# Modulation partials summed over partitions with ones as weights, in four column groups of TensorE

## What is computed

```
# first block, layer l
ada = silu(c) @ w_ada[l] + b_ada[l]                 # (1, 6 * 1024)
sh1, sc1, g1, sh2, sc2, g2 = split(ada, 6)
h = x * (1 + sc1) + sh1
...
# second block, layer l: 9 * 1024 columns, for two vectors
mod_x = ada_params(c, w_ada[l], b_ada[l])           # for the tokens
mod_c = ada_params(c_ctx, w_ada[l], b_ada[l])       # for the context
```

## Time and profile before

| | us |
|---|---|
| median of 3 runs | 2823.49 |
| lowest and highest | 2822.88, 2828.95 |
| the profiled execution | 2827.61 |
| its span | 2825.8 |
| DVE busy in it | 1769.0 |
| ACT busy in it | 1086.2 |
| POOL busy in it | 226.9 |

### The profile page before, as it was taken

One profiled execution on the slowest core, in us unless ns is written; L12 is line 12 of the kernel. 1 busy time (PEld: TensorE's weight loads), 2 busy tenths in 40 slices (PEclk: granted clock), 3 DMA queues, 4 the chain that ended last, 5 costly groups with the idle time before them and its releaser, 6 DMA issues. The chain is left out here.

```text
span 2825.8 us, 40791 instructions
## 1 busy us (share of the span) xinstructions
PE 2630.3 (93%) x15939; PEld 2259.5 (80%) x15939; DVE 1769.0 (63%) x3184; ACT 1086.2 (38%) x2068; POOL 226.9 (8%) x170
## 2 busy tenths in 40 slices
PE   4768999999998999999999999999999999989999
PEld 4748998968998688887765778888788888777999
DVE  6567776657777656545759675554555533668754
ACT  2243544444443433323338233322333322446553
POOL 2000100001000211101000021110111100100110
PEclk8868999868999999999999999999999999999999
DMA  8924874914765244332620334433244433522653
GB/s 295 261 89 139 265 250 151 271 46 152 238 230 186 75 135 148 131 123 90 164 88 2 120 100 154 135 127 112 91 148 145 138 124 116 147 75 84 215 176 124
DMA packets 354873, 413.80 MB, mean 146 GB/s; under 512 B 24737, under 2 KB 291914, under 8 KB 354618
## 3 DMA queue, kind: packets, MB, share of 16 engines
q1 hardware_dynamic: 352496, 404.13, 44.8%
q0 software_dynamic: 832, 4.65, 0.5%
q10 hardware_dynamic: 1354, 2.43, 0.2%
HBM read 409.56 MB, written 5.27 MB: 147 GB/s over the span
## 5 line engine op out<-in xcount | busy, mean ns | idle before, releaser
L683 DVE TENSOR_TENSOR weight_lo<-raw_weights,weight_hi 128x512 fp32r<-128x512 f32 x1024 | 774.6, 763 | 886.0 <-ACT weight_hi L1242 873.9
L1242 ACT ACTIVATE weight_hi<-raw_weights 128x512 fp32r<-128x512 f32 x1024 | 635.6, 631 | 1326.7 <-PE bank L895 1203.9
L895 PE MATMUL bank<-H_hi,weight_hi 128*128 128x256 f32 (+1 forms) x2832 | 967.6, 342 | 71.3 <-POOL H_lo L853 46.3
L895 PE MATMUL bank<-H_lo,weight_hi 128*128 128x256 f32 (+1 forms) x2832 | 947.8, 335 | 0.0
L895 PE MATMUL bank<-H_hi,weight_lo 128*128 128x256 f32 (+1 forms) x2832 | 947.4, 335 | 0.0
L895 PEld LDWEIGHTS bank<-H_hi,weight_hi 128*128 128x128 f32 x2832 | 548.9, 194 | 156.9 <-issue 75.9
L895 PEld LDWEIGHTS bank<-H_hi,weight_lo 128*128 128x128 f32 x2832 | 549.5, 194 | 50.6
L895 PEld LDWEIGHTS bank<-H_lo,weight_hi 128*128 128x128 f32 x2832 | 550.2, 194 | 47.7 <-issue 1.0
L1545 DVE SCALAR_TENSOR_TENSOR ada_partial<-raw_weights,silu_c,ada_partial 128x512 f32<-128x512 f32 x616 | 441.1, 743 | 1.7 <-issue 0.4
L895 PE MATMUL bank<-hidden_hi,weight_hi 128*128 128x256 f32 (+1 forms) x1056 | 358.7, 340 | 3.2 <-DVE weight_lo L683 3.2
L895 PE MATMUL bank<-hidden_hi,weight_lo 128*128 128x256 f32 (+1 forms) x1056 | 354.9, 336 | 0.0
(11 more groups left out here) (172 smaller groups left out, 2169.4 us busy)
## 6 DMA issues: line engine op xcount, KB each, us to landing
raw_weights<-in_w_ada_dram SPq DMA_DIRECT2D x120, 1024.0 KB, 5.3
raw_weights<-in_w_ffn_up_dram SPq DMA_DIRECT2D x88, 1024.0 KB, 5.5
raw_weights<-in_w_ffn_in_dram SPq DMA_DIRECT2D x44, 1024.0 KB, 5.9
raw_weights<-in_w_ffn_down_dram SPq DMA_DIRECT2D x32, 1024.0 KB, 5.2
raw_weights<-in_w_in_dram SPq DMA_DIRECT2D x18, 1024.0 KB, 6.0
raw_weights<-in_w_ffn_out_dram SPq DMA_DIRECT2D x16, 1024.0 KB, 7.7
raw_weights<-in_w_in_ab_dram SPq DMA_DIRECT2D x12, 1024.0 KB, 10.0
raw_weights<-in_w_in_cd_dram SPq DMA_DIRECT2D x12, 1024.0 KB, 8.2
```

Of the source, the lines that this page charges most:

```text
L683: eng.tensor_tensor(WL[:, p.g % SPLIT, 0:p.kt * CW].rearrange("p (t n) -> p t n", n=CW), raw_ap(ch.n, ch.kt, CW)[:, p.k0:p.k0 + p.kt, :], ...
L895: return pe.matmul(o, w, x, start=start, stop=stop, skip_group_check=True)
L1242: act.activation(WH[:, p.g % SPLIT, 0:p.kt * CW].rearrange("p (t n) -> p t n", n=CW), raw_ap(ch.n, ch.kt, CW)[:, p.k0:p.k0 + p.kt, :], ACT ...
```

## The change

`sum_rows` swaps the operands and the layout. The stationary operand is now a block of ones, 32 columns wide, and the partials are moved, 128 of them per call. Each of the four calls of a vector writes into its own 32 partitions of the bank, 32q to 32q + 31: the columns 32q to 32q + 31 of each of the four blocks of 128. So every one of these 32 partitions holds the same sums, lying along the free axis. The number of calls stays at 4 or 8.

`columns` turns them upright. A tensor_reduce with a transpose inside blocks of 32 x 32 adds up the 32 equal rows and puts the 32 results on the partitions, into the first 4 or 8 columns of the group's own `ACC`, which is free by then. DVE waits for its end (`chain.link`), and then a scalar_tensor_tensor multiplies by 1/32 and adds the bias.

```diff
--- before.py
+++ after.py
@@ -917,10 +917,11 @@
             if g > 0:
 
                 pe.wait_ge(ada_out, g)
-            for j in range(AW // P):
-                for v in range(nv):
-                    ins = mm(B_ADA[:, j * nv + v:j * nv + v + 1],
-                             ACC[:, g % 2, v, j * P:(j + 1) * P], ones[:, 0:1], True, True)
+            for v in range(nv):
+                part = ACC[:, g % 2, v, :].rearrange("p (j q i) -> p j q i", q=4, i=32)
+                for q in range(4):
+                    o = B_ADA[32 * q:32 * q + 32, P * v:P * v + P].rearrange("p (j i) -> p j i", i=32)
+                    ins = mm(o, ones[:, 0:32], part[:, :, q, :], True, True)
             ins.then_inc(ada_sum, 1)
 
         def wait_bank(at, f):
@@ -1571,12 +1572,16 @@
             bias = (B1 if m < 2 else B2)[:, m % 2, :]
             dve.wait_ge(ada_sum, g + 1)
             b = bias[:, n * at:n * at + n]
+            col = ACC[:, g % 2, 0, 0:n * nv]
+            chain.link(dve.tensor_reduce(col, B_ADA[:, 0:P * nv].rearrange("p (c i) -> p c i", i=32), AX.X, ALU.add,
+                                         apply_transpose=True))
             if nv == 2:
                 b = b[:, :, None].broadcast_to([P, n, 2])
-                o, i = AD[m][:, n * at:n * at + n, :], B_ADA[:, 0:2 * n].rearrange("p (c v) -> p c v", v=2)
+                o, i = AD[m][:, n * at:n * at + n, :], col.rearrange("p (v c) -> p c v", v=2)
             else:
-                o, i = AD[m][:, n * at:n * at + n, 0], B_ADA[:, 0:n]
-            dve.tensor_tensor(o, i, b, ALU.add).then_inc(ada_out, 1)
+                o, i = AD[m][:, n * at:n * at + n, 0], col
+            dve.scalar_tensor_tensor(out=o, in0=i, scalar=1.0 / 32, in1=b, op0=ALU.mult, op1=ALU.add
+                                     ).then_inc(ada_out, 1)
 
         def setup():
             dve.memset(ZERO[:, :], 0.0)
```

## The result

The kernel with the change takes 2804.64 us (median of 5 runs, 2795.43 to 2807.25) where the kernel before took 2828.94 in the runs beside it (5 runs, 2822.88 to 2832.91): a ratio of 0.9911, with an interval of 0.9889 to 0.9934, or 19 to 31 us less. Two later repetitions gave 0.9889 and 0.9907. The forecast of 2796 is a ratio of 0.9903 to the 2823.49 it started from. The profiled execution has a span of 2802.8 us, 23.0 less than before.

The account below looks back on a forecast made before the run. PE was taken to bound the kernel; 30.5 us saved on its sums less 2.3 paid on DVE made 28.2 off the 2825.8 us span, 2797.6, hence a forecast median of 2796, range 2789 to 2811.

Parts of the forecast that it names:

- The sum on PE: In 20 one-vector and 23 two-vector modulation sums: 0.34 and 1.03 us saved each, 30.5 us together.
- the lower end of the range: 2789 us: a third of the layout cost absent in the 43 sums, 43 x 0.15 = 6.5 us.
- Rival 1: In the sums on PE: records no faster than 0.053 us each, saving 14.1 in all, 2809.4 us; chance 0.15.
- Rival 2: In every sum: four calls not run at once, 12.0 us lost on PE, 2.3 on DVE, 2837.8; chance 0.05.
- The reduce: On DVE in each group: a plain reduce's time, adding 0.45 or 0.32 us, 22.8 us of work in all.
- rival 3: In the DVE loop: a reduce takes 1.7 us rather than 0.42, costing 8.8, 2801.8 us; chance 0.10.
- Where DVE sets the time: From 738 to 862 us, DVE's loop pays the reduce in full: 5 x 0.45 = 2.3 us.
- The attention entries: Before attention stages: PE waits for the last column step, but the shorter sum's 0.34 or 1.03 covers 0.32 or 0.45.
- The DVE work outside the DVE-bound cycles: Mostly hidden in the counted stretches, behind PE's cover of three weight pieces: 4.3 us at 256 columns, 8.2 at 512.

Follow-up runs that it names:

- no_reduce: The kernel after without the transposing reduce and the factor 1/32, DVE adding the bias to the bank's first columns; 2794.20 us, ratio 0.9872.
- reduce_only: The kernel before with the transposing reduce and its wait added on DVE, PE's sum left as it was; 2834.21 us, ratio 1.0030.

## Why the prediction was right, and where it was off

**The sum on PE** (1.79 to 0.76, 0.88 to 0.54). Right: 0.78 and 0.55. Both parts of it were seen apart: passes of four records some 0.11 us apart, and 0.30 us per visit with narrow weights (0.26 to 0.30 by the cycles), where the prediction had 0.33. Measured from sum to sum the saving is 0.96, not 1.03, and 0.33, not 0.34: 23 x 0.07 + 20 x 0.01 = 1.8 us less than forecast. Two of the prediction's figures don't come out of its rows, without harm to the forecast: a record of the old sum costs 1.79 / 16 = 0.112 us and not 0.106, and the 0.15 us at the lower end of the range is nearly half of the layout cost and not a third.

**The rivals on PE.** Rival 1, records at 0.053 us each, is refuted: sixteen of them span 0.64 us. The Trainium skill gives a floor of about 25 ns from start to start (TensorE: Matmul & The Clock Gate, Wait — 56ns, not 53.3ns?). Between calls into different column groups the trace doesn't bear it out: two records run in the window 1043.08:1043.09 and four in 1043.10:1043.11, so four starts lie within 0.03 us. Only the mean over the passes, one record per 0.027 us, is near it. Rival 2 did not happen, but the run with one column group showed its price: 42.6 us from the kernel after, against 42.5 in the prediction (30.5 + 12.0).

**The reduce.** Forecast as a plain one, 419 and 285 ns; the groups of DVE after (busy us, mean ns, idle before):

```profile
L1576 DVE TRANSPOSE_TENSOR_REDUCE ada_partial<-bank 128x8 f32<-128x256 f32 x28 | 12.3, 439 | 0.0
...
L1576 DVE TRANSPOSE_TENSOR_REDUCE ada_partial<-bank 128x4 f32<-128x128 f32 x32 | 9.9, 309 | 2.5 <-PE bank L895 1.8 <-DVE X L1728 0.2
```

That is 20 and 24 ns over these (the plain reduce of 128 elements read SBUF, this one PSUM), and rival 3 falls. The Trainium skill's one element per cycle and lane for the transposing array (Vector Engine (DVE) Microarchitecture Reference, The reshape front-end and per-opcode configuration) fits the trace as far as it goes: 128 elements more take 130 ns more, about 1 ns each.

**Where DVE sets the time.** Right in place and mechanism, a little small in size: 0.57 us per cycle on average instead of 0.45. The timeline shows 0.49 of it, the reduce and the gap to the instruction that waits for its end; the other 0.08 isn't traced. The four cycles that repeat make 2.3 us. A fifth like them would make it 2.8 where the prediction had 2.3, but the stretch from sum 27 to 29 doesn't show it (132.40 to 133.59 us before, 132.14 to 134.36 after).

**The attention entries.** Wrong. The prediction let the shorter sum pay for the reduce there. PE's timeline after, at two of these places:

```profile
1460.48 1.99 PE L895 MATMUL bank<-k,q 64*128 64x512 f32 x8 [2.27 <-DVE ada L1583]
...
2504.18 3.65 PE L895 MATMUL bank<-k,q 64*128 64x512 f32 x8 [2.13 <-DVE ada L1583]
```

Before, PE waited 1.78 us at both for the values' copies on ACT; the second place then:

```profile
2526.10 1.99 PE L895 MATMUL bank<-k,q 64*128 64x512 f32 x8 [1.78 <-ACT v L1373]
```

The sum had long been done, so its length didn't count; DVE comes to the columns only behind its low part, and the step is now the last to arrive: 0.49 and 0.35 us more.

The two entries of the first block pay as well, though the profile names ACT's copy there. Before and after, DVE's column step and then PE:

```profile
576.56 0.15 DVE L1579 TENSOR_TENSOR ada<-bank,b_ada_cols 128x4 f32<-128x4 f32 x1
576.81 0.93 PE L895 MATMUL bank<-k,q 64*128 64x128 f32 x8 [1.63 <-ACT v L1373]
```

```profile
572.55 0.16 DVE L1583 SCALAR_TENSOR_TENSOR ada<-ada_partial,b_ada_cols 128x4 f32<-128x4 f32 x1
572.82 0.93 PE L895 MATMUL bank<-k,q 64*128 64x128 f32 x8 [1.98 <-ACT v L1374]
```

PE starts 0.10 and 0.11 us behind the end of the column step, and 0.4 to 0.8 behind the end of the copy: here the step was the last to arrive even before. The wait is longer by 0.35. At the other entry (sum 8) the sum does stand right ahead of it, as the prediction had it, and the wait went from 0.84 to 1.62 us: 0.42 for the shorter sum, which PE can't use, and 0.36 for the reduce. In no_reduce the four waits are 1.26, 1.62, 1.78 and 1.78 us. So the reduce costs about 1.5 us at the four entries, where the prediction had nothing. With four reduces the longest of these waits is 3.7 us, as the step's length on the path demands.

**Together.** 30.5 - 1.8 - 2.3 - 1.5 = 24.9 us by the measured terms (24.4 with a fifth DVE-bound cycle), and about 25 in the profiles without the stage whose clock varies; the prediction had 28.2. The three timed ratios make 25, 31 and 26 us of 2824. The close agreement of the sum is worth less than it looks: the three regular stretches hold 20 of the 23 two-vector and 8 of the 20 one-vector sums and show 21.9 us, and in the other stretches terms of a few tenths stand beside chance of several us.

The DVE work outside the DVE-bound cycles was called hidden, and one reduce is nearly so (no_reduce's median is 3.8 us lower, less than the two intervals can tell apart; 2.3 and 1.5 make 3.8). What the prediction didn't say is how thin the cover is at 256 columns; it took three pieces of weights as 4.3 us, and the fourfold reduce found 0.4 left behind the first.

**Left open.** Why reduce_only pays 8 us, 2 to 15 by its interval, where the traced terms add up to 4.6 to 6.5; whether taking the columns late is a gain of 2 us; and what decides how long PE stays at 1.2 GHz in the second layer's attention.

## What to carry to other kernels

An fp32 record cost PE 0.11 us, whether it loaded 128 columns and moved one, loaded 32 and moved 128, or loaded and moved 128; with a narrow block of ones as weights, four such records in four column groups cost one, and a vector engine can turn the result upright for about 0.3 to 0.45 us. Each visit with such narrow weights cost some 0.3 us, however many calls it held, so calls of this kind are best put together (not tried here). A swap of operands without the column groups gained nothing. An operation added to the helper engine is free only where that engine waits for PE: look for cycles in which it waits for a load that its own last read starts, and put the operation behind that read.

## What was unexpected

After 4.2 us of idling by PE in two waits, the granted clock was at 0.50 for anything between some 10 and 50 us in all, in a stage whose products are the same in all these kernels: 86.67 to 103.53 us, and for the kernel after alone 92.41 to 103.53, which is nearly half of what this change gained. A difference of the spans of two single profiles is worth little here; stage by stage, the cycles at full clock repeat within 0.01 us.

An engine busy for 18.0 of 23.58 us had 0.4 us of room left per cycle. The share of busy time didn't show it; four times the disputed operation did.
